# A second mixer's delta rule and block attention placed between the units of its own projection GEMM

## The reference, cut to what is touched

```python
def hybrid_mixer(x, norm_g, w_in, gdn_conv_w, a_log, dt_bias, gdn_norm_g, moba_norm_g, rel_bias, w_out):
    h = rmsnorm_2(x, norm_g)
    proj = h @ w_in                      # 2048 -> 3072 (qkv_a) + 1024 (z) + 16 (b, a) + 3072 (qkv_b)
    qkv_a = jax.nn.silu(causal_dwconv(qkv_a, gdn_conv_w))
    q_a, k_a, v_a = [to_heads(t, 8) for t in jnp.split(qkv_a, 3, axis=-1)]
    beta = jax.nn.sigmoid(b_a)
    g = -jnp.exp(a_log) * jax.nn.softplus(a_a + dt_bias)
    o_a = gated_delta_rule(l2norm(q_a), l2norm(k_a), v_a, g, beta)
    o_a = rmsnorm_2(o_a, gdn_norm_g) * jax.nn.silu(z_a)
    o_b = moba_attention(q_b, k_b, v_b, rel_bias)      # one block of 256: causal, with relative bias
    o_b = rmsnorm_2(o_b, moba_norm_g)
    return jnp.concatenate([o_a, o_b], axis=-1) @ w_out
```

## Time and profile before

| | us |
|---|---|
| median of 3 runs | 2773.63 (2773.52 to 2780.64) |
| the profiled execution | 2775.24 |
| its span, first to last instruction | 2773.5 |
| TensorE busy (share of span) | 2583.9 (93%) |
| VectorE busy | 1687.7 (61%) |
| ScalarE busy | 1278.5 (46%) |
| GpSimd busy | 19.3 (1%) |
| mean granted TensorE clock | 0.957 |

### The profile page before, as it was taken

One profiled execution on the slowest core, in us unless ns is written; L12 is line 12 of the kernel. 1 busy time (PEld: TensorE's weight loads), 2 busy tenths in 40 slices (PEclk: granted clock), 3 DMA queues, 4 the chain that ended last, 5 costly groups with the idle time before them and its releaser, 6 DMA issues.

```text
span 2773.5 us, 36912 instructions
## 1 busy us (share of the span) xinstructions
PE 2583.9 (93%) x14342; PEld 2222.7 (80%) x14342; DVE 1687.7 (61%) x2185; ACT 1278.5 (46%) x1646; POOL 19.3 (1%) x40
## 2 busy tenths in 40 slices
PE   6999597999999999979999878899799999999997
PEld 5878386888888888868878557788688888888886
DVE  5899565665565644455685435376676676675454
ACT  4445555544444444454444422355454444444342
POOL 0000000000000000000010000000000000000000
PEclk9999699999999999999999858999999999999999
DMA  6553053555555555535565300155356555655563
GB/s 205 174 152 107 0 168 121 183 193 185 187 191 184 194 183 182 185 129 177 194 198 195 116 0 1 40 166 185 120 162 194 183 193 184 191 187 189 166 207 121
DMA packets 235786, 436.15 MB, mean 157 GB/s; under 512 B 14232, under 2 KB 32680, under 8 KB 235552
## 3 DMA queue, kind: packets, MB, share of 16 engines
q1 hardware_dynamic: 232368, 424.02, 47.3%
q0 software_dynamic: 2160, 6.44, 0.7%
q10 hardware_dynamic: 1152, 4.19, 0.4%
HBM read 432.51 MB, written 3.69 MB: 157 GB/s over the span
## 4 chain that ended last, share of the span: by engine, by line
PE 87%; DVE 8%; ACT 3%; issue 2%; DMA 1%; DVEq 0%; SPq 0%; ACTq 0%
PE ps L740 50%; PE ps L743 25%; DVE w_lo L429 2%; PE ps L1372 1%; DVE ar L1134 1%; PE ps L1158 1%; PE ps L1352 1%; PE ps L1729 1%; PE ps L726 1%; PE ps L728 1%; PE ps L729 1%; PE ps L1726 1%; PE ps L1205 1%; PE ps L977 1%; PE ps L1720 1%
## 5 line engine op out<-in xcount | busy, mean ns | idle before, releaser
L740 PE MATMUL ps<-x,w_hi 128*128 128x512 f32 x4704 | 1495.6, 400 | 67.4 <-DVE x L878 28.3
L429 DVE TENSOR_TENSOR w_lo<-w_raw,w_hi 128x1024 fp32r<-128x1024 f32 (+3 forms) x820 | 986.3, 1208 | 782.5 <-ACT w_hi L423 780.4
L423 ACT ACTIVATE w_hi<-w_raw 128x1024 fp32r<-128x1024 f32 (+3 forms) x820 | 852.5, 1045 | 1003.9 <-PE ps L743 942.6
L743 PEld LDWEIGHTS ps<-x,w_lo 128*128 128x128 f32 x4704 | 892.3, 190 | 210.9
L743 PE MATMUL ps<-x,w_lo 128*128 128x256 f32 x4704 | 931.3, 280 | 0.0
L740 PEld LDWEIGHTS ps<-x,w_hi 128*128 128x128 f32 x4704 | 725.1, 191 | 73.8 <-issue 54.9
L740 PE MATMUL ps<-h,w_hi 128*128 128x512 f32 x1408 | 443.4, 396 | 5.0 <-DVE w_lo L429 5.0
L743 PEld LDWEIGHTS ps<-h,w_lo 128*128 128x128 f32 x1408 | 264.7, 188 | 62.2
L743 PE MATMUL ps<-h,w_lo 128*128 128x256 f32 x1408 | 276.9, 278 | 0.0
L740 PEld LDWEIGHTS ps<-h,w_hi 128*128 128x128 f32 x1408 | 214.6, 189 | 6.0 <-DVE w_lo L429 5.8
L465 ACT ACTIVATE half<-ps 128x512 f32<-128x512 f32 x182 | 106.6, 592 | 108.4 <-PE ps L743 108.4
(11 more groups left out here) (295 smaller groups left out, 1634.0 us busy)
## 6 DMA issues: line engine op xcount, KB each, us to landing
w_raw<-in_w_gate SPq DMA_DIRECT2D x88, 1024.0 KB, 5.2
w_raw<-in_w_up SPq DMA_DIRECT2D x88, 1024.0 KB, 5.2
w_raw<-in_w_down SPq DMA_DIRECT2D x88, 1024.0 KB, 5.1
w_raw<-in_w_in SPq DMA_DIRECT2D x80, 1024.0 KB, 5.1
w_raw<-in_w_out SPq DMA_DIRECT2D x32, 1024.0 KB, 5.1
w_raw<-in_w_xkv SPq DMA_DIRECT2D x8, 1024.0 KB, 5.1
w_raw<-in_w_uq SPq DMA_DIRECT2D x18, 256.0 KB, 3.6
w_raw<-in_w_ukv SPq DMA_DIRECT2D x16, 256.0 KB, 4.1
```

Source lines behind the costliest of these rows:

```text
L423: nc.scalar.activation(w_hi[:, u % HIS, 0:ks.stop - ks.start, cs], w_raw[:, slot(g, j), ks, cs], ACT.Copy)\
L429: nc.vector.tensor_tensor(w_lo[:, slot(g, j), ks, cs], w_raw[:, slot(g, j), ks, cs], w_hi[:, u % HIS, 0:ks.stop - ks.start, cs].bitcast(F3 ...
L740: nc.tensor.matmul(bank, w_h(k, cs), x(k).rearrange("p a n -> p (a n)"), start=(n == 0 and k == 0), stop=False)
L743: ins = nc.tensor.matmul(bank[:, T:2 * T], w_l(k, cs), x(k)[:, 0, :], start=False, stop=(final and k == ks.stop - 1))
```

## The change

The projection is cut anew. `qkv_a` has one turn: q's 1024 columns, then the b and a columns, then k and v. The rest of the projection (q and k of the block attention, its v, and z last) is one GEMM, `mix2b`, of 8 groups and 64 units, in the narrow form (v stays in swap form), in which a unit is 24 matmuls of 256 columns into two PSUM banks; narrow groups take turns on banks 0-1 and 2-3, and banks 4 to 7 belong to the filler. VectorE evicts a narrow group straight from PSUM, two operations, without ScalarE.

TensorE gets a filler: before each unit of `mix2b` but the first it runs one step of `mixer_pe`, 63 steps, and the same steps stand in `mixer_dve` and `mixer_act` (there step j follows the split of unit j+2, and step 1 stands ahead of unit 4's split). Steps 1 to 7: l2 norm and bias row; 8 to 15: decays, k k', q k'; 16 to 18: transposes of v, k and the first inverse; 19 to 35: levels 1 to 6, as three steps each (W, UW, and transposes of U in place of TW and the T update; the last level has no third); 36 to 39: u, w, state and output; 41 to 44: the delta rule's head norm; 45 to 62: block attention, two steps for each head; and behind the last unit 8 selector matmuls. The two banks are 4-5 and 6-7 for the two halves.

The convolution moves from `z_ba` and `qkv_b` to a filler of `qkv_a`. The level masks and the mask of q k' are multiplied on GpSimd (`gdn_pool`), 18 operations of 128x1024. ScalarE copies T after the transposes. The masks' DMA moves up on GpSimd's queue, and the 16 DMAs that bring the bias back move behind the level masks. `ahead` takes a filler too, and behind `mix2b` the preparation of x for `w_out_2` goes in two halves, with silu(z) in two halves; `w_out_2` takes its rows in plain order. TensorE's steps 45 to 62 call `attn_scores`, `attn_turn` and `attn_weigh`, which are the old loop body cut in three.

```diff
-            Gemm("qkv_a", 3, [group(w_loop(A["w_in_2"], 0 + b * P, 2 * W), 4, out=(ar, ZA + b, 8))
-                        for b in (0, 4)], x2c, rs_x),
-            Gemm("z_ba", 1, [group(w_cols(A["w_in_2"], 3072, W), 4, out=(ar, ZZ, 0)),
-                             group(w_cols(A["w_in_2"], 3584, W), 4, out=(ar, ZZ + 4, 0)),
-
-                             group(w_cols(A["w_in_2"], 4096, 128), 4, at=[0], out=(ar, BA, 0))], x2c, rs_x),
-            Gemm("qkv_b", 1, [group(w_cols(A["w_in_2"], 4112 + k * W, W), 4, out=(ar, ZB + 4 * k, 0)) for k in range(4)] +
-                             [group(w_cols(A["w_in_2"], 4112 + (4 + k) * W, W), 4, out=(ar, VN2 + 2 * k, H // 2), kind="v") for k in range(2)],
-                 x2c, rs_x, column=1),
-            Gemm("w_out_2", 2, [group(turned(w_loop(A["w_out_2"], b * P, 2 * W)), 4, out=(xt, 0 + b, 8), kind="add")
-                        for b in (0, 4)], lambda k: x2c((k + 8) % DC)),
+            Gemm("qkv_a", 1, [group(w_cols(A["w_in_2"], W * c, W), 4, out=(ar, ZA + 4 * c, 0)) for c in range(2)] +
+
+                             [group(w_cols(A["w_in_2"], 4096, 128), 4, at=[0], out=(ar, BA, 0))] +
+                             [group(w_cols(A["w_in_2"], W * c, W), 4, out=(ar, ZA + 4 * c, 0)) for c in range(2, 6)],
+                 x2c, rs_x),
+            Gemm("mix2b", 1, [group(w_cols(A["w_in_2"], 4112 + k * W, W), 4, out=(ar, ZB + 4 * k, 0)) for k in (0, 2, 1, 3)] +
+                             [group(w_cols(A["w_in_2"], 4112 + (4 + k) * W, W), 4, out=(ar, VN2 + 2 * k, H // 2), kind="v") for k in range(2)] +
+                             [group(w_cols(A["w_in_2"], 3072 + k * W, W), 4, out=(ar, ZZ + 4 * k, 0)) for k in range(2)],
+                 x2c, rs_x, form="narrow", column=1),
...
+                    if filler and u:
+                        next(filler)
...
+            if filler:
+                finish(filler)
...
-        SUM_BANK = {name: 3 if name in ("q", "kv", "mean", "ln", "conv", "mix", "ff", "final") else 7 for name in STATS}
+        SUM_BANK = {name: 3 if name in ("q", "kv", "mean", "ln", "conv", "mix", "ff", "mix2", "final") else 7 for name in STATS}
...
+            yield from idle(4)
+            yield from gconv_taps(dve, 0)
+            yield from idle(8)
+            yield from gconv_taps(dve, 1)
+            yield from idle(4)
+            for b in range(2, 5):
+                yield from idle(4)
+                yield from gconv_taps(dve, b)
...
+        gp = Milestones(sem("gdn_pool"), ["B00", "B01", "qk0", "qk1"] + [f"B{l}{s}" for l in levels for s in range(2)])
...
+        def gdn_pool(pool):
+            def level(l, s):
+                gp.reach(nc.gpsimd.tensor_tensor(bb_[s], part(at_, s), mask(l, NP // 2), ALU.mult), f"B{l}{s}")
+            pool.wait_ge(mask_in, 16)
+            for s in range(2):
+                gv.wait(pool, f"at{s}")
+                level(0, s)
+            for s in range(2):
+                gv.wait(pool, f"qk{s}")
+                gp.reach(nc.gpsimd.tensor_tensor(part(qk_, s), part(qk_, s), mask(7, NP // 2), ALU.mult), f"qk{s}")
+            for s in range(2):
+                gv.wait(pool, f"U0{s}")
+                level(1, s)
+            for l in levels:
+                if l < LV - 1:
+                    for s in range(2):
+                        gt.wait(pool, f"W{l}{s}")
+                        level(l + 1, s)
...
+            def decays(s):
+                gt.wait(dve, f"G_rows{s}")
+                for h in range(4 * s, 4 * s + 4):
+                    for c in range(2):
+                        ins = ts(dt_[:, 2 * h + c, :], pb(6, 2)[:, 2 * h + c - 8 * s, :],
+                                 G_nat[:, c, 8 + h:9 + h], 0.0, ALU.subtract, ALU.min)
+                        if (h, c) != (4 * s + 3, 1):
+                            dve_chain.step(ins)
+                dve_chain.sync(dve)
+                gv.reach(ins, f"dt{s}")
...
+            for l in levels:
+                yield
+                for s in range(2):
+                    gt.wait(dve, f"UW{l}{s}")
+                    gv.reach(tt(part(uu_, s), part(uu_, s), pb(4 + 2 * s, 2), ALU.subtract), f"U{l}{s}")
+                yield
+                if l < LV - 1:
+                    yield
+
...
             for h in range(H):
+                attn_bias(dve, a, h)
+                yield
+                attn_norm(dve, a, h)
+                yield
...
+                    gs.reach(copy(part(ww_, s), pb(4 + 2 * s, 2)), f"W{l}{s}")
+                yield
+                yield
+                if l < LV - 1:
+                    for s in range(2):
+                        gt.wait(act, f"TR{l}{s}")
+                        gs.reach(copy(part(tt_, s), pb(4 + 2 * s, 2)), f"T{l}{s}")
+                    yield
...
-                    for n in range(8 * s, 8 * s + 8):
-                        last = mm(pb(0)[:, n, :], bb_[:, n, :], tt_[:, n, :], start=True, stop=True)
+                    gp.wait(pe, f"B{l}{s}")
+                    gs.wait(pe, f"T{l - 1}{s}")
+                    for n in half_of(s):
+                        last = mm(pb(4)[:, n, :], bb_[s][:, n - 8 * s, :], tt_[:, n, :], start=True, stop=True)
                     gt.reach(last, f"W{l}{s}")
+                yield
                 for s in range(2):
                     gs.wait(pe, f"W{l}{s}")
-                    if l < LV - 1:
-                        for n in range(8 * s, 8 * s + 8):
-                            last = mm(pb(4)[:, n, :], uu_[:, n, :], ww_[:, n, :], start=True, stop=True)
-                        gt.reach(last, f"TW{l}{s}")
-                    for n in range(8 * s, 8 * s + 8):
-                        last = mm(pb(0)[:, n, :], ww_[:, n, :], uu_[:, n, :], start=True, stop=True)
+                    for n in half_of(s):
+                        last = mm(pb(4)[:, n, :], ww_[:, n, :], uu_[:, n, :], start=True, stop=True)
                     gt.reach(last, f"UW{l}{s}")
+                yield
+                if l < LV - 1:
+                    for s in range(2):
+                        gv.wait(pe, f"U{l}{s}")
+                        turned(s, f"TR{l}")
+                    yield
...
+            for h in range(H):
+                attn_turn(pe, a, h)
+                if h + 2 < H:
+                    attn_scores(pe, a, h + 2)
+                yield
+                if h % 4 == 0:
+                    pe.wait_ge(evicted, e0 + 10 + 2 * (h // 4))
+                attn_weigh(pe, a, h)
+                yield
+            yield
+            next(hn)
+            yield
...
-            run_("qkv_a", stat=["mix2"])
-            ahead_("z_ba")
-            dve.wait_ge(*groups_out("qkv_a")())
-            filler = gconv_dve(dve)
-            run_("z_ba", filler)
-            rel_dve(dve)
-            ahead_("qkv_b")
-            run_("qkv_b", filler)
-            ahead_("w_out_2")
-            dve.wait_ge(rel_back, 16 * 2 * H)
-            row = ar[0:16, RQK, :]
-            l2 = headnorm_dve(dve, "l2", l2_src, 16, 1.0, row, extra=P ** -0.5)
-            attention_dve(dve, ATTN["moba"], l2)
-            finish(l2)
-            finish(headnorm_dve(dve, "moba", moba_src, 8, 1 / P, row))
-            gdn_dve(dve)
-            finish(headnorm_dve(dve, "gdn", og_src, 8, 1 / P, row, None,
-                                lambda: prep_dve(dve, "moba", moba_src, lambda c: col("moba_norm"))))
-            gs.wait(dve, "silu_z")
-            dve.wait_ge(hn_used, 16)
-            nc.vector.tensor_tensor(span(og_src, 0, H), span(og_src, 0, H), ar[:, ZZ:ZZ + H, :], ALU.mult)\
-                .then_inc(applied, 1)
-            prep_dve(dve, "gdn", og_src, lambda c: col("gdn_norm"))
+            run_("qkv_a", gconv_dve(dve), 1, stat=["mix2"])
+            ahead_("mix2b")
+            filler = mixer_dve(dve)
+            next(filler)
+            run_("mix2b", filler)
+            ahead_("w_out_2", filler=filler)
+            prep_dve(dve, "gdn", og_src, lambda c: col("gdn_norm"), None, 0, 4)
+            hn = headnorm_dve(dve, "moba", moba_src, H, 1 / P, rows_hn)
+            next(hn)
+            next(hn)
+            gated(dve, 1)
+            prep_dve(dve, "gdn", og_src, lambda c: col("gdn_norm"), None, 4, 4)
+            finish(hn)
+            prep_dve(dve, "moba", moba_src, lambda c: col("moba_norm"))
...
-            multiply(pe, G["z_ba"])
-
-            pe.wait_ge(evicted, G["qkv_b"].e0 - 2)
-            rel_pe(pe)
-            pe.wait_ge(rel_sb, 1)
-            multiply(pe, G["qkv_b"])
-            pe.wait_ge(evicted, G["w_out_2"].e0)
-            rows = ar[0:16, RQK, :]
-            l2 = headnorm_pe(pe, "l2", 16, 8, rows)
-            attention_pe(pe, ATTN["moba"], [lambda e: e.wait_ge(*all_evicted("qkv_b")()), lambda e: e.wait_ge(*groups_out("qkv_b")())], l2)
-            finish(l2)
-            pe.wait_ge(o_kept, 2 * H)
-            pe.wait_ge(biased, 2 * H)
-            finish(headnorm_pe(pe, "moba", 8, 16, rows))
-            pe.wait_ge(hn_used, 12)
-            gdn_pe(pe)
-
```

(49 more changed lines are left out.)

825 lines of the change are left out of this document (481 added, 344 removed).

## The result

The changed kernel takes 2669.22 us (median of 4 runs, 2666.86 to 2675.11) against 2773.57 us before (4 runs): ratio 0.9625 [0.961, 0.964], 104.4 us less. Measured again in a later set it took 2673.0 us (5 runs, 2670.44 to 2673.69) against 2772.75: ratio 0.9632 [0.9616, 0.9648]. The forecast was 2654 us, 119 less, in a range of 2642 to 2692; the first median lies 1.2 us above the narrower band of 2647 to 2668 that it gave a chance of 0.62. The profiled execution of after is the slowest of its four, 2675.11 us, with a span of 2673.3 us; against the 2775.24 us of before it is 100.1 us less.

The account below looks back on a forecast made before the run. TensorE bounds the kernel, with one long hole from 1525 to 1800 us. 114.0 + 11 + 0 - 2.5 - 3.5 = 119.0 us off 2775.24 gives 2656.2, as median about 2654 us, range 2642 to 2692.

Parts of the forecast that it names:

- What bounds the kernel: TensorE's GEMMs bound the kernel almost throughout, except one long hole from 1525 to 1800 us where its clock falls.
- what the hole is worth: Between qkv_b's last matmul and unit 4 of w_out_2: 242.4 us without GEMM work, less 128.4 of filler, gives back 114.0.
- The filler: TensorE's own work for the steps moved between mix2b's units, counted by instruction at full clock: 128.4 us.
- Narrow form, 0 us: 48 mix2b units of 24 matmuls at 0.115 us last 2.76 us, same as wide; bounds 2 us gain, 84 us loss.
- Convolution out of the short units, 11 us back: At 1400 to 1432 us, quarter units wait behind convolution taps; moving the taps into qkv_a recovers 64 missing matmuls' time.
- No wait for a low part in the b and a units: Sign expected in the profile after: qkv_a's short b and a units no longer wait for their weights' low parts.
- New waits, 2.5, and the ends, 3.5: Allowances in the new stage: 0.1 us for each of some 25 tight steps, and 3.5 us for start and end.
- Level masks, 0: 18 masks on GpSimd at 1.2 to 4.9 us each, hidden under up to 6.8 us of cover; 0 taken.
- leaks: Rival: steps don't hide as reckoned, 0.5 us for each of 63, 31 us more: 2685 us (2668 to 2700); chance 0.14.
- VectorE held by GpSimd: Rival: VectorE's splits or updates wait up to one GpSimd mask each, 0 to 34 us more; chance 0.06 for over 2668.
- Clock: Rival: TensorE idles a little in every step and the stage runs at half clock: 2954 us, slower than before; chance 0.03.
- In name only: Rival: GEMM units wait for the steps in full; 54.5 us of TensorE's idle time in the hole stays: 2708 us; chance 0.05.

## Why the prediction held, and where it was short

- *What bounds the kernel* and *what the hole is worth*: right. With the steps behind the units, 0.999 of the old time; between them, 0.963.
- *The filler*: right, 127.56 us for 128.4. Counting instructions by kind and taking each kind's spacing from the steady stretches of before gave it within 1%, though nothing stood in it for the edges of the 16-row groups.
- *Narrow form, 0 us*: this term failed, by 10.4 us. It was sized from one pair of neighbours (0.11 us) and from the 128-column steps (0.112); the form's own spacing is 0.120 us, and each unit that follows a step starts with 0.08 more. The text named 0 to -2 and +84 as bounds, and 0 was taken without anything for the switch between forms. The loads do overlap, as it argued. The mean unit, 3.00 us, stands at the very bound from which the text called itself wrong, and the level cycle, 17.50, inside its bound of 18. The switch is the larger part: 24 x 0.120 would be 2.88 us a unit, 4.8 us in all, and the other 5.6 come where a unit meets a step.
- *Swapped units*: they weren't in the sum. 1.9 us for 16 of them, probably by the same switch, which wasn't taken apart here.
- *Convolution out of the short units, 11 us back*: the idea that the taps were the cause was in part wrong. "No wait for a low part in the b and a units" didn't come true: 3 us stay, with 3.4 us at half clock behind them, and they go with the short tiles wherever these stand.
- *New waits, 2.5, and the ends, 3.5*: near in sum (6.8 for 6.0), by luck, and wrong in place. In the steps nothing waits; what was paid is the 3 us before the stage and the half clock at its end, which stood in no term.
- *Level masks, 0*: right. There are 16, not the 18 of the text. They take 2.70 us in the mean, inside 1.2 to 4.9 and under the cover of 6.8; ten of them take 2.38 to 2.42 and the others up to 3.40. The Trainium skill (GPSIMD Engine Reference, section 3.1) led to an estimate of 2.3 us, near those ten. The Trainium skill (SBUF — State Buffer, section Who interferes with whom) says that a GpSimd operation and a VectorE operation with two SBUF inputs shut each other out; the traces agree (3.44 us for a split at 1462.6 in after, 1.21 for the update with one input in PSUM right behind it).
- *The rivals*: none decided, though by number alone 2669.2 lies where leaks (2668 to 2700) or a held VectorE were to show. Leaks: no idle time in 293 us. Clock: 1.00 in the stage. VectorE held by GpSimd: splits are 10% longer on average and nobody waits; with twice the masks its mechanism is real and costs 7 us. In name only: it takes steps placed behind the units to get there.
- *Outside the stage*: about 5 us are given back, 4.1 of them in cross attention under half clock. The forecast had no term for it, and its cause stays open.

In the profiled executions, of the 119.0 us forecast 106.8 came in the stage; 1.1 were lost ahead of it, 4.8 behind unit 4 and 0.9 around the span, which leaves 100.1. That execution is the slowest of four, and the medians give 104.4.

## What to carry to other kernels

When a bound engine idles in a stage of small dependent steps, place the steps one by one between units of work that depend on none of them: one unit is the cover of one step, and pairing the steps cost a quarter of the gain. Cost the change as the bound engine's own instruction spacings, each form measured in its own steady run, plus a price for each switch between forms, since once the waits are gone these spacings are all there is. Look for half clock where the engine is busy, too, and see what its matmuls look like there; here the ones with 16 rows cost clock where they stood close together, and 0.39 us a group at full clock.

## What the runs showed of the hardware

- Matmuls of 16 rows go with a falling clock though TensorE is busy: 0.50 over 41 us with the engine busy 35.7, and 0.83 after the same matmuls were given 128 rows, 112 of them zero. The Trainium skill (TensorE: Matmul & The Clock Gate, section What's actually happening) puts the clock down to how busy the engine has been; these runs show that busy time as a profile counts it isn't all of it. In the changed kernel groups of eight such matmuls between units leave the clock at 1.00. Within a group the number of rows doesn't change the spacing at full clock, 0.216 us for both, but a group of eight with 16 rows costs 0.39 us more at its edges (4.99 us for 4.60, unit included).
- A narrow fp32r matmul of 256 columns with its own weight load stands 0.120 us behind the last one, in runs and between steps; an fp32 one of 128 columns 0.109; and the first narrow matmul behind 128-column fp32 ones costs 0.08 more.
- A VectorE operation with two inputs in SBUF takes 3.4 us in place of 1.2 while GpSimd runs its products back to back (2.4 to 3.4 us each in the run with every mask twice), 2.26 (L1714 of after) where only one of them meets it; one with an input in PSUM keeps its 1.21.
